# A five-block transformer in 32-bit: split projections against projections on the operands as they land

## The chip, the cores and the metric

The kernel runs on one core of one Trainium2 chip, as one launch. The metric is the time of that launch on the device in microseconds, the median over repeated runs; lower is better. Inputs, weights and output are 32-bit floating point.

## The reference

`x` has 256 tokens of 1024 features. It passes four layers, each a mixer and a gated feed-forward part (2816 wide), and then a fifth block with its own context of 256 tokens. In each layer six vectors of 1024 come from a matrix-vector product, and they shift, scale and gate:

```
mod = silu(c) @ ada_w[i] + ada_b[i]                  # 1024 x 6144, 24 MB
sh1, sc1, g1, sh2, sc2, g2 = split(mod, 6)
h = rms_norm(x, gain) * (1 + sc1) + sh1
x = x + g1 * mixer_i(h)                              # stick-breaking, MoBA, sliding window, stick-breaking
h = rms_norm(x, gain) * (1 + sc2) + sh2
x = x + g2 * ((silu(h @ w_gate) * (h @ w_up)) @ w_down)
```

The fifth block modulates `x` and the context, projects both with `w_in_2`, runs window attention and a bidirectional gated delta rule, joins them through `w_br_attn_2`, `w_br_dn_2`, `w_out_2`, and ends in `relu(h @ w_mlp1_2)^2 @ w_mlp2_2`. All weights are 32-bit and each is read once; the page counts 390 MB of reads.

## The kernel before

**Units.** Every projection is cut into units. A unit is one transfer of four blocks of 128 x 512 weights (1 MB) into a slot of the ring `raw`, and the matrix products of these four blocks with both tiles of 128 tokens: eight products (activation block 128 x 128 as the loaded weights of TensorE, the weights' 128 x 512 streamed). A few units are narrower (256 or 32 columns) or have two blocks. `units` and `loads` (lines 595 to 661) are lists that are written at build time: which units, and in which order SP fetches them, mixed with the "ada" loads, 1 MB each, of the modulation matrices.

**The split.** In the feed-forward parts, the two stick-breaking mixers and the fifth block, a unit is multiplied in three products of a reduced 32-bit type (`F32R`). ACT writes a rounded copy `w_hi` of the slot (`convert`, line 925, the copy is L939), DVE the remainder `w_lo` (`convert`, its subtraction is L1443), and only then is the slot of `raw` given back (`raw_free`). There are two buffers of each. The activations are split alike: ACT writes `full`, then `h_hi` or `act_hi` (`split`, L965), DVE `h_lo` or `act_lo` (L1516), on semaphores `split_full`, `split_hi`, `split_lo`. PE then does, per block (`unit`, line 2149):

```
nc.tensor.matmul(banks[t][:, 0:n], x_hi[:, kt, ts], w_hi[:, u % 2, i, 0:n], start=st, stop=False)
nc.tensor.matmul(banks[t][:, 0:n], x_hi[:, kt, ts], w_lo[:, u % 2, i, 0:n], start=False, stop=False)
ins = nc.tensor.matmul(banks[t][:, 0:n], x_lo[:, kt, ts], w_hi[:, u % 2, i, 0:n], start=False, stop=en)
```

These are L2161, L2162 and L2163; `half_unit` in the stick-breaking mixer does the same on two blocks (L2414 to L2416). A unit of eight blocks-times-tiles is thus 24 products.

**The native form.** In the MoBA and the sliding-window mixer the units are multiplied as 32-bit operands straight from `raw` (`unit_as_landed`, L2367, and L2462 for the output projection). One such product leaves two records in the trace: the program has 64 of L2462, the trace 128.

**Modulation.** DVE accumulates `acc += ada_row_block * c` over the eight blocks of a third of a modulation matrix (L1496, 1 MB per operation; `acc_c` for the context), `modulation_units`, line 1483. PE then sums over the partitions with a product against ones (`modulation` of PE, L2209 for the gates, L2219 for the columns), ACT copies the result. Which accumulations stand between which units is in the tables `ADA_MIX` and `ADA_FF`: `ADA_MIX[l]` by unit of the mixer, `ADA_FF[l]` by unit of the feed-forward part.

**Order.** Each engine's program is written out by hand and runs in that order. SP: `loads` in order, each waiting until its slot of the ring (`RING = 4`) is free: for a native unit when PE is done, else when DVE has read it. DVE: conversions, accumulations, the elementwise steps of attention (`SB_SLOTS`, `MOBA_DVE`, `SWA_DVE`), residuals and norms, interleaved by unit. Between layers stands a norm: residual (L1588, L1594), squares on ACT, scale on DVE (`n_st`, L1553), 32 transposes on PE (L2177, L2184), modulation on ACT (L1004). Ahead of the fifth block SP waits until the fourth layer's last residual is written before it fetches the context and masks.

Of the kernel before, what the change touches and what calls it, by code (L numbers as in the profile page):

```python
# [10 lines left out]
F32 = mybir.dt.float32  # L11
F32R = mybir.dt.float32r
# [5 lines left out]
P = 128  # L18
# [10 lines left out]
RING = 4  # L29
# [21 lines left out]
class Walk:  # L51


    def __init__(self):
# [4 lines left out]
        self.low = 0  # L59
        self.native = 0  # L60
# [46 lines left out]
def build(nc, w, out):  # L107
    with ExitStack() as ctx:
# [18 lines left out]
        w_hi_t, w_hi_off = at("w_hi", 2 * 2048, F32R)  # L127
        w_hi = w_hi_t[:, :].rearrange("p (s k n) -> p s k n", s=2, k=UNIT_K)
        w_lo_t, w_lo_off = at("w_lo", 2 * 2048, F32R)
        w_lo = w_lo_t[:, :].rearrange("p (s k n) -> p s k n", s=2, k=UNIT_K)  # L130
        x_res = tile("x_res", NT * D).rearrange("p (t d) -> p t d", t=NT)
        h_hi_t, h_off = at("h_hi", KT * SEQ, F32R)
        h_hi = h_hi_t[:, :].rearrange("p (k n) -> p k n", k=KT)
        h32 = tile("h32", KT * SEQ, offset=h_off).rearrange("p (k n) -> p k n", k=KT)
        h_lo = tile("h_lo", KT * SEQ, F32R).rearrange("p (k n) -> p k n", k=KT)
        act_hi_t, act_hi_off = at("act_hi", FFT * SEQ, F32R)
        act_hi = act_hi_t[:, :].rearrange("p (k n) -> p k n", k=FFT)
        act32 = tile("act32", KT * SEQ, offset=act_hi_off).rearrange("p (k n) -> p k n", k=KT)
        act_lo_t, act_lo_off = at("act_lo", FFT * SEQ, F32R)
        act_lo = act_lo_t[:, :].rearrange("p (k n) -> p k n", k=FFT)  # L140
        gates = tile("gates", 2 * D).rearrange("p (g n) -> p g n", g=2)
        full_t, full_off = at("full", 2 * 512)
        full = full_t[:, :].rearrange("p (b n) -> p b n", b=2)
# [42 lines left out]
        v_st = tile("v_st", 2 * NT * 512, offset=act_lo_off + 8 * 1024).rearrange("p (b t n) -> p b t n", b=2, t=NT)  # L186
        rope_st = tile("rope_st", NT * 512, offset=act_hi_off + 8 * 1024).rearrange("p (t n) -> p t n", t=NT)
        aT_odd = tile("aT_odd", 3 * 512, offset=act_hi_off + 12 * 1024).rearrange("p (b n) -> p b n", b=3)
        rot_st = tile("rot_st", NT * 512, offset=act_hi_off + 18 * 1024).rearrange("p (t n) -> p t n", t=NT)
# [32 lines left out]
        AH, AL, AB, AC = act_hi_off, act_lo_off, acc_off, qk_off  # L222
# [26 lines left out]
        q_decT, u_st = by_round("q_decT", h_off), by_round("u_st", h_off + 8 * KB)  # L249
# [14 lines left out]
        hi_ready = sem("hi_ready")  # L264
        lo_ready = sem("lo_ready")
# [35 lines left out]
        split_full = sem("split_full")  # L301
        split_hi = sem("split_hi")
        split_lo = sem("split_lo")
# [112 lines left out]
        ADA_U = 3 * KT  # L416

# [91 lines left out]
        LAT_F = DEPTH * (2 * (KT // 2) + 4 + FF // 256) + KT  # L509
# [60 lines left out]
        ADA_MIX = [{}, {n: [(1, 2 * KT + i)] for i, n in enumerate((0, 1, 3, 5, 7, 9, 11, 13))}, {}, {}]  # L570
        FF_FREE = [n for n in range(2, 32) if n not in (20, 21, 22, 23)]
        ADA_FF = [{}, {}, {}, {}]
        for i in range(2 * KT):
            ADA_MIX[0].setdefault((0, 0, 1, 2, 3, 4, 5, 5, 6, 7, 8, 9, 10, 11, 12, 13)[i], []).append((0, KT + i))
        for l in range(DEPTH):
            twice = KT if l + 1 == LAT else 0
            count = ADA_U - sum(len(x) for x in ADA_MIX[l + 1].values()) if l + 1 < LAT else ADA_U
            for i in range(count):
                slot = 2 + (i + min(i, twice)) * 29 // (ADA_U + twice) if count == ADA_U else FF_FREE[i * len(FF_FREE) // count]
                ADA_FF[l].setdefault(slot, []).append((l + 1, i))  # L580

# [20 lines left out]
        def add(m, pieces, kts, what="unit"):  # L602
            units.append((what, [(c0, mm, c1, n) for c0, mm, c1, n in pieces], list(kts), sum(p[3] for p in pieces)))

        mixer_units = []
        for l in range(DEPTH):
            kind, w_in, w_out = mixer(l)
            form = "unit" if kind == "sb" else "native"
            for what, g, pieces in qkv_panels(kind):
                for h in range(2):  # L610
                    add(w_in, [(c0, w_in, c1, n) for c0, c1, n in pieces], range(4 * h, 4 * h + 4), form)
            for h in range(2):
                for n in range(2):
                    add(w_out, [(0, w_out, 512 * n, 512)], range(4 * h, 4 * h + 4), form)
# [25 lines left out]
        def more_units(n, n_mix):  # L640

            return 0 if n == 0 else 2 if n == n_mix - 1 else 1

# [4 lines left out]
        loads += [next(ahead), next(ahead)]  # L648
        for l in range(DEPTH):
            small.setdefault(len(loads), []).append(("mixer", l))  # L650
            n_mix = 2 * len(qkv_panels(KINDS[l])) + 4
            for n in range(n_mix):
                loads += [next(ahead) for _ in range(more_units(n, n_mix))]
                loads += [("ada", *a) for a in ADA_MIX[l].get(n, [])]
            for p in range(FF // 256):
                for pos in range(2 * p - 1 if p else 0, 2 * p + 1):
                    loads.append(next(ahead))
                    loads += [("ada", *a) for a in ADA_FF[l].get(pos, [])]
# [16 lines left out]
        def freed_by_dve(upto):  # L675

            return sum(load[0] != "native" for load in loads[:upto])
# [2298 lines left out]
```

## Time and profile before

| | us |
|---|---|
| median of 3 runs (2114.25 to 2118.66) | 2116.64 |
| profiled execution, span from first to last instruction | 2113.7 |
| median less span: what lies around it | 2.9 |
| PE busy | 1926.3 |
| DVE busy | 1342.8 |
| ACT busy | 917.3 |

The page gives no time of its own for the profiled execution beside the span; the 2.9 us are the median's excess over the span. A busy PE is not PE at its peak: records of consecutive products overlap, since a record holds a product's latency as well. What a product costs in a stream is read from the distance between the starts of two neighbours.

### The profile page before, as it was taken

The numbers are of one execution on the slowest core, as the hardware profiler recorded it, in microseconds if no ns is written. First come the engines' busy times: TensorE is split into PE (matmuls) and PEld (weight loads), VectorE is DVE, ScalarE is ACT, GpSimd is POOL, SyncE is SP. The second block draws the span as 40 slices with busy tenths as digits, with TensorE's granted clock in tenths as the row PEclk, the third lists the DMA queues.
The fourth block names the chain that finished last, engine by engine and source line by source line (L and its number), as shares of the span: only waits on it lengthen the run. The fifth ranks groups of instructions, "written<-read, shape, count | busy, mean of one in ns | idle before, by whom it ended". The sixth has DMA issues, their size and how long they took to land.

```text
span 2113.7 us, 33128 instructions
## 1 busy us (share of the span) xinstructions
PE 1926.3 (91%) x13890; PEld 1500.4 (71%) x13890; DVE 1342.8 (64%) x1412; ACT 917.3 (43%) x1367; POOL 112.5 (5%) x139
## 2 busy tenths in 40 slices
PE   4888999999899998899999898998999888798999
PEld 3666887655687764687777677777777777776877
DVE  6776775563587734588755578875537645366465
ACT  3555444332544334544355554435435321335443
POOL 1001000110100000100000100001000302000000
PEclk9998999999999999999999999998989999999999
DMA  8763886564599931599933367983123000234552
GB/s 321 287 224 116 277 284 238 202 209 144 186 338 313 334 104 60 169 338 316 343 112 122 116 201 257 320 307 131 58 86 120 2 4 4 83 111 150 172 185 102
DMA packets 215401, 393.37 MB, mean 186 GB/s; under 512 B 11337, under 2 KB 130133, under 8 KB 199893
## 3 DMA queue, kind: packets, MB, share of 16 engines
q1 hardware_dynamic: 214741, 391.12, 54.0%
q8 instruction: 111, 1.82, 0.4%
q14 instruction: 37, 0.30, 0.0%
q0 software_dynamic: 512, 0.13, 0.0%
HBM read 390.17 MB, written 1.05 MB: 185 GB/s over the span
## 4 chain that ended last, share of the span: by engine, by line
PE 57%; DVE 24%; ACT 10%; issue 6%; DMA 2%; POOL 0%; DVEq 0%; ACTq 0%; SPq 0%; POOLq 0%
PE G L2161 12%; PE G L2163 11%; PE G L2162 11%; DVE w_lo L1443 11%; PE G L2367 6%; DVE acc L1496 5%; ACT w_hi L939 5%; PE G L2462 2%; PE A L2756 2%; ACT full L1004 1%; PE G L2770 1%; DMA raw<-in_ffn_w_down 1%; DVE act_st L1781 1%; PE A L2768 1%; DVE n_st L1553 1%
## 5 line engine op out<-in xcount | busy, mean ns | idle before, releaser
L1443 DVE TENSOR_TENSOR w_lo<-raw,w_hi 128x2048 fp32r<-128x2048 f32 (+2 forms) x237 | 513.4, 2166 | 285.4 <-ACT w_hi L939 274.8
L939 ACT CAST w_hi<-raw 128x2048 fp32r<-128x2048 f32 (+1 forms) x230 | 427.7, 1860 | 532.7 <-PE G L2163 479.8
L2161 PE MATMUL G<-w_hi,h_hi 128*128 128x512 f32 (+2 forms) x1232 | 491.3, 399 | 29.6 <-DVE w_lo L1443 12.1
L2163 PE MATMUL G<-w_hi,h_lo 128*128 128x512 f32 (+2 forms) x1232 | 480.9, 390 | 0.0
L2162 PE MATMUL G<-w_lo,h_hi 128*128 128x512 f32 (+2 forms) x1232 | 480.6, 390 | 0.0
L1496 DVE SCALAR_TENSOR_TENSOR acc<-raw,c_col,acc 128x2048 f32<-128x2048 f32 x120 | 282.0, 2350 | 43.3 <-DMA raw<-in_ada_w 22.5
L2161 PEld LDWEIGHTS G<-w_hi,h_hi 128*128 128x128 f32 x1232 | 235.0, 191 | 85.1 <-issue 40.0
L2163 PEld LDWEIGHTS G<-w_hi,h_lo 128*128 128x128 f32 x1232 | 234.1, 190 | 49.3
L2162 PEld LDWEIGHTS G<-w_lo,h_hi 128*128 128x128 f32 x1232 | 235.4, 191 | 45.1
L2161 PE MATMUL G<-w_hi,act_hi 128*128 128x512 f32 (+2 forms) x624 | 243.8, 391 | 24.0 <-DVE w_lo L1443 21.6
L2163 PE MATMUL G<-w_hi,act_lo 128*128 128x512 f32 (+2 forms) x624 | 241.0, 386 | 0.0
L2162 PE MATMUL G<-w_lo,act_hi 128*128 128x512 f32 (+2 forms) x624 | 240.8, 386 | 0.0
L2161 PEld LDWEIGHTS G<-w_hi,act_hi 128*128 128x128 f32 x624 | 118.8, 190 | 54.0 <-issue 28.4
L2163 PEld LDWEIGHTS G<-w_hi,act_lo 128*128 128x128 f32 x624 | 118.8, 190 | 23.7
L2162 PEld LDWEIGHTS G<-w_lo,act_hi 128*128 128x128 f32 x624 | 119.0, 191 | 22.6 <-issue 0.2
L2367 PE MATMUL G<-raw,h 128*128 128x512 f32 (+1 forms) x288 | 119.7, 572 | 0.0
L2367 PEld LDWEIGHTS G<-raw,h 128*128 128x128 f32 x288 | 54.4, 192 | 57.3 <-issue 56.5
L1516 DVE TENSOR_TENSOR act_lo<-full,act_hi 128x512 fp32r<-128x512 f32 (+1 forms) x78 | 52.1, 678 | 52.0 <-ACT act_hi L965 43.5
L2219 PE MATMUL A<-consts,acc 128*128 128x1 f32 x320 | 40.9, 262 | 23.6 <-DVE acc L1496 23.6
L2219 PEld LDWEIGHTS A<-consts,acc 128*128 128x128 f32 x320 | 41.7, 211 | 25.6 <-DVE acc L1496 23.8
L2462 PE MATMUL G<-raw,act 128*128 128x512 f32 x128 | 56.7, 593 | 0.0
L1004 ACT ACTIVATE full<-A,mod,gsc 128x128 f32<-128x128 f32 (+1 forms) x108 | 45.3, 489 | 21.6 <-DVE gsc L1532 13.7
(402 smaller groups left out, 2097.4 us busy)
## 6 DMA issues: line engine op xcount, KB each, us to landing
raw<-in_ada_w SPq DMA_DIRECT2D x96, 1024.0 KB, 5.1
raw<-in_ffn_w_gate SPq DMA_DIRECT2D x88, 512.0 KB, 4.0
raw<-in_ffn_w_up SPq DMA_DIRECT2D x88, 512.0 KB, 5.1
raw<-in_ffn_w_down SPq DMA_DIRECT2D x40, 1024.0 KB, 5.2
raw<-in_w_mlp SPq DMA_DIRECT2D x32, 1024.0 KB, 5.3
raw<-in_w_ada SPq DMA_DIRECT2D x24, 1024.0 KB, 5.4
raw<-in_w_in SPq DMA_DIRECT2D x18, 1024.0 KB, 5.3
raw<-in_sb_w_in SPq DMA_DIRECT2D x32, 512.0 KB, 4.8
```

What stands on the lines that cost most here:

```text
L939: nc.scalar.copy(w_hi[:, c % 2, 0:len(kts), 0:n], raw[:, slot].rearrange("p (k n) -> p k n", k=UNIT_K)[:, 0:len(kts), 0:n])\
L1004: return nc.scalar.activation(dst, src, ACT.Identity, scale=gsc[:, l % 2, gain + c:gain + c + 1], bias=mod[:, l % 2, which + c:which + c + 1])
L1443: return nc.vector.tensor_tensor(w_lo[:, c % 2, ks, 0:n], raw[:, slot].rearrange("p (k n) -> p k n", k=UNIT_K)[:, ks, 0:n], w_hi[:, c % 2, ...
L1496: nc.vector.scalar_tensor_tensor(out=acc_of(l, j), in0=raw[:, slot], scalar=c_col[:, c:c + 1], in1=acc_of(l, j), op0=ALU.mult, op1=ALU.add ...
L1516: nc.vector.tensor_tensor(dst_lo, full[:, f % 2, 0:n * dst_lo.shape[1]].rearrange("p (a n) -> p a n", n=n), dst_hi.bitcast(F32), ALU.subtr ...
L2161: nc.tensor.matmul(banks[t][:, 0:n], x_hi[:, kt, ts], w_hi[:, u % 2, i, 0:n], start=st, stop=False)
L2162: nc.tensor.matmul(banks[t][:, 0:n], x_hi[:, kt, ts], w_lo[:, u % 2, i, 0:n], start=False, stop=False)
L2163: ins = nc.tensor.matmul(banks[t][:, 0:n], x_lo[:, kt, ts], w_hi[:, u % 2, i, 0:n], start=False, stop=en)
L2219: ins = nc.tensor.matmul(banks[0][:, i:i + 1], x[:, c * P:c * P + P], ones[:, 0:1], start=True, stop=True)
L2367: ins = nc.tensor.matmul(banks[t][:, 0:n], h32[:, kt, t * P:t * P + P], raw[:, slot].rearrange("p (k n) -> p k n", k=UNIT_K)[:, i, 0:n], s ...
L2462: ins = nc.tensor.matmul(G[2 * (po[n] % 2) + t], act32[:, 2 * j + i, t * P:t * P + P], raw[:, slot].rearrange("p (k n) -> p k n", k=UNIT_K ...
L2756: ins = nc.tensor.matmul(A[c][half_of(1 - ch), cols_of(h)], LT[half_of(ch), c, cols_of(h)], X[half_of(ch), c, cols_of(h)], start=True, sto ...
```

## The change

- `convert` and `split` are gone on ACT and DVE, with `w_hi`, `w_lo`, `h_lo`, `act_lo` and their semaphores. ACT writes `hT` or `actT` in one operation (`put`), semaphore `panel_in`.
- PE's `unit` waits for the landed slot and does one product per block and tile, on 32-bit operands, for every projection: all are in the native form.
- The ring has seven slots. A unit's slot is free when PE is done with it, an ada load's when DVE is.
- The ada loads stand elsewhere: 16 of the 24 of a layer are accumulated in its own mixer (8 in the sliding-window layer), the first 8 (or 16) in the feed-forward part before; before, 16 stood in the first mixer, 8 in the second and none in the others. The last 8 of the fifth block are accumulated beside its first four units (`ADA_LAT`).
- Some tiles of the fifth block (`X`, `wu`, `u_st`) get a place of their own, `solve`.

```diff
-RING = 4
+RING = 7
...
+        ADA_MIX, ADA_FF, ADA_LAT = [{}, {}, {}, {}], [{}, {}, {}, {}], {}
+        for l, slots, own in ((0, 14, 2 * KT), (1, 14, 2 * KT), (2, 8, KT), (3, 14, 2 * KT)):
+            for i in range(own):
+                ADA_MIX[l].setdefault(i * slots // own, []).append((l, ADA_U - own + i))
+        for l, slots, ahead in ((0, 30, KT), (1, 30, 2 * KT), (2, 30, KT), (3, 22, 2 * KT)):
+            for i in range(ahead):
+                ADA_FF[l].setdefault(2 + i * slots // ahead, []).append((l + 1, i))
+        for i in range(KT):
+            ADA_LAT.setdefault(i // 2, []).append((LAT, 2 * KT + i))
...
-            def split(dst_hi, emit_full):
-                f, b = k.f, k.low
+            def put(ins):
                 k.f += 1
-                k.low += 1
-                if b >= 2:
-                    act.wait_ge(split_lo, b - 1)
-                n = dst_hi.shape[-1]
-                emit_full(full[:, b % 2, 0:n * dst_hi.shape[1]]).then_inc(split_full, 1)
-                act.wait_ge(split_full, f + 1)
-                nc.scalar.copy(dst_hi, full[:, b % 2, 0:n * dst_hi.shape[1]].rearrange("p (a n) -> p a n", n=n)).then_inc(split_hi, 1)
+                ins.then_inc(panel_in, 1)
...
-            def unit(x_hi, x_lo, kts, banks, first, last, n=512, done=gemm_done, ready=None, tiles=False):
-
-                u = nth_converted[k.u]
-                k.u += 1
-                pe.wait_ge(hi_ready, u + 1)
-                pe.wait_ge(lo_ready, u + 1)
+            def weights(slot):
+
+                return raw[:, slot].rearrange("p (k n) -> p k n", k=UNIT_K)
+
+            def unit(x, kts, banks, first, last, n=512, done=gemm_done, ready=None, tiles=False, again=False):
+
+                if not again:
+                    k.u += 1
+                    k.load = k.next_load(loads, "unit")
+                slot, count, _ = k.load
+                pe.wait_ge(landed[slot], count)
                 for t in range(NT):
-                    ts = slice(t * P, t * P + P)
                     if ready is not None:
-                        pe.wait_ge(split_lo, ready[t] - k.native)
+                        pe.wait_ge(panel_in, ready[t])
                     for i, kt in enumerate(kts):
-                        st = first and i == 0
-                        en = last and i == len(kts) - 1
-                        nc.tensor.matmul(banks[t][:, 0:n], x_hi[:, kt, ts], w_hi[:, u % 2, i, 0:n], start=st, stop=False)
-                        nc.tensor.matmul(banks[t][:, 0:n], x_hi[:, kt, ts], w_lo[:, u % 2, i, 0:n], start=False, stop=False)
-                        ins = nc.tensor.matmul(banks[t][:, 0:n], x_lo[:, kt, ts], w_hi[:, u % 2, i, 0:n], start=False, stop=en)
+                        ins = nc.tensor.matmul(banks[t][:, 0:n], x[:, kt, t * P:t * P + P], weights(slot)[:, i, 0:n],
+                                               start=first and i == 0, stop=last and i == len(kts) - 1)
```

Three places show how the engines' programs move. The first is DVE in the first layer's feed-forward part: `act_st` is the product of gate and up, `acc` the modulation sums. Before:

```order
L1443 TENSOR_TENSOR w_lo<-raw,w_hi 128x2048 x2
L1781 TENSOR_TENSOR act_st<-G,silu_st 128x256 x2
L1443 TENSOR_TENSOR w_lo<-raw,w_hi 128x2048
L1516 TENSOR_TENSOR act_lo<-full,act_hi 128x512
L1496 SCALAR_TENSOR_TENSOR acc_101<-raw,c_col,acc_101 128x2048
L1443 TENSOR_TENSOR w_lo<-raw,w_hi 128x2048
L1781 TENSOR_TENSOR act_st<-G,silu_st 128x256 x2
```
and now, the same stretch:

```order
L1346 SCALAR_TENSOR_TENSOR acc_97<-raw,c_col,acc_97 128x2048
L1603 TENSOR_TENSOR act_st<-G,silu_st 128x256 x4
L1346 SCALAR_TENSOR_TENSOR acc_97<-raw,c_col,acc_97 128x2048
L1603 TENSOR_TENSOR act_st<-G,silu_st 128x256 x4
L1346 SCALAR_TENSOR_TENSOR acc_97<-raw,c_col,acc_97 128x2048
```
All conversions and splits have left it, and fewer accumulations stand between the `act_st`. An `act_st` row now stands for two panels where nothing comes between them.

The second is SP at the start of the fifth block (`in_w_in` are its units, `in_w_ada` its modulation loads, `in_ctx` the context, which waits for the last residual of layer four). Before:

```order
L765 DMA raw<-in_w_in 128x4x512 x2
L765 DMA raw<-in_w_in 128x4x256
L736 DMA ctx_raw<-in_ctx 128x2x1024
L737 DMA mask_st<-in_masks 128x1216
L738 DMA rope_cs<-in_rope 128x4x64
L739 DMA rope_g<-in_q_norm_g 128x64
L740 DMA rope_g<-in_k_norm_g 128x64
L741 DMA sinks<-in_attn_sink 128x8
L742 DMA dn_rows<-in_a_log 128x16
L743 DMA dn_rows<-in_dt_bias 128x16
L744 DMA dn_rows<-in_dn_norm_g 128x64
L765 DMA raw<-in_w_in 128x4x256
```
and now:

```order
L734 DMA raw<-in_w_in 128x4x512
L705 DMA ctx_raw<-in_ctx 128x2x1024
L706 DMA mask_st<-in_masks 128x1216
L707 DMA rope_cs<-in_rope 128x4x64
L708 DMA rope_g<-in_q_norm_g 128x64
L709 DMA rope_g<-in_k_norm_g 128x64
L710 DMA sinks<-in_attn_sink 128x8
L711 DMA dn_rows<-in_a_log 128x16
L712 DMA dn_rows<-in_dt_bias 128x16
L713 DMA dn_rows<-in_dn_norm_g 128x64
L738 DMA raw<-in_w_ada 128x2048 x2
L734 DMA raw<-in_w_in 128x4x512
```
Only one unit is fetched ahead of the context now, not three, and two ada loads stand between the first unit and the second.

The third is DVE behind the context's norm, in the same place (`aq` is the query panel, `ss` its squared sums). Before:

```order
L1553 TENSOR_SCALAR n_st<-ctx_raw,rms_t 128x1024
L1443 TENSOR_TENSOR w_lo<-raw,w_hi 128x4x256
L1532 SCALAR_TENSOR_TENSOR gsc<-mod,cols 128x8
L1516 TENSOR_TENSOR act_lo<-full,act_hi 128x4x128 x2
L1443 TENSOR_TENSOR w_lo<-raw,w_hi 128x4x256
L1516 TENSOR_TENSOR act_lo<-full,act_hi 128x512 x2
L1828 TENSOR_REDUCE ss_84<-lrot 128x16
L1523 TENSOR_SCALAR rms_v<-ss_84 128x16
```
and now (the rows after these, up to the rotated `aq`, are as before, and two more `acc` rows stand behind them):

```order
L1395 TENSOR_SCALAR n_st<-ctx_raw,rms_t 128x1024
L1374 SCALAR_TENSOR_TENSOR gsc<-mod,cols 128x8
L1346 SCALAR_TENSOR_TENSOR acc<-raw,c_col,acc 128x2048 x6
L1634 TENSOR_REDUCE ss_80<-lrot 128x16
L1365 TENSOR_SCALAR rms_v<-ss_80 128x16
```
Six accumulations now stand ahead of the query's norm and two behind it; all eight are due before PE can sum the block's gates.

## Rows read from the trace of the kernel before

**Rows 1.** The page: span; busy time by engine; GB/s in 40 slices.
```profile
span 2113.7 us, 33128 instructions
...
PE 1926.3 (91%) x13890; PEld 1500.4 (71%) x13890; DVE 1342.8 (64%) x1412; ACT 917.3 (43%) x1367; POOL 112.5 (5%) x139
...
GB/s 321 287 224 116 277 284 238 202 209 144 186 338 313 334 104 60 169 338 316 343 112 122 116 201 257 320 307 131 58 86 120 2 4 4 83 111 150 172 185 102
```
**Rows 2.** Timeline, PE: start, length (us), engine, line, operation, tiles, shapes.
```profile
1463.01 0.28 PE L2161 MATMUL G<-w_hi,h_hi 128*128 128x256 f32 x1
...
1468.65 0.28 PE L2163 MATMUL G<-w_hi,act_lo 128*128 128x256 f32 x1
...
1870.05 0.39 PE L2161 MATMUL G<-w_hi,act_hi 128*128 128x512 f32 x1
...
1884.79 0.39 PE L2163 MATMUL G<-w_hi,act_lo 128*128 128x512 f32 x1
```
**Rows 3.** Chain that ended last, in order of time: start, length (us), work.
```profile
399.76 27.47 PE G L2367 x64
...
428.10 6.87 PE G L2367 x16
```
**Rows 4.** Groups by shape, PE: count, busy us, mean ns, idle before, releasers.
```profile
L2161 PE MATMUL G<-w_hi,h_hi 128*128 128x512 f32 x1200 | 482.5, 402 | 29.6 <-DVE w_lo L1443 12.1 <-issue 8.8 <-DVE h_lo L1516 8.5
...
L2161 PE MATMUL G<-w_hi,act_hi 128*128 128x512 f32 x592 | 234.2, 396 | 22.9 <-DVE w_lo L1443 21.6 <-ACT dz L1235 1.1
...
L2414 PE MATMUL G<-w_hi,act_hi 128*128 128x512 f32 x16 | 6.6, 415 | 1.5 <-DVE act_lo L1516 1.1 <-DVE w_lo L1443 0.4
```
**Rows 5.** Waits of PE: who waited for whom, us in total, times, longest.
```profile
PE G L2161 <- DVE w_lo L1443: 33.7, 22, 3.3
PE A L2177 <- DVE n_st L1553: 27.4, 13, 4.2
PE A L2219 <- DVE acc L1496: 23.6, 1, 23.6
PE G L2161 <- issue: 8.8, 6, 2.0
PE G L2161 <- DVE h_lo L1516: 8.5, 14, 1.3
...
PE A L2497 <- DVE act_st L1781: 6.2, 6, 3.0
...
PE A L2904 <- DVE hid_st L2105: 3.5, 8, 0.5
```
**Rows 6.** Timeline in the first mixer, DVE and PE.
```profile
52.42 2.29 DVE L1443 TENSOR_TENSOR w_lo<-raw,w_hi 128x2048 fp32r<-128x2048 f32 x1 [0.22 <-DVE acc L1496]
...
54.81 0.47 PE L2161 MATMUL G<-w_hi,h_hi 128*128 128x512 f32 x1 [1.23 <-issue]
```
**Rows 7.** Timeline of the norm behind the second mixer, DVE.
```profile
543.74 1.21 DVE L1443 TENSOR_TENSOR w_lo<-raw,w_hi 128x1024 fp32r<-128x1024 f32 x1
...
545.10 0.16 DVE L1543 SCALAR_TENSOR_TENSOR rms_v<-ssq,ssum 128x1 f32<-128x1 f32 x1 [0.15 <-DVE w_lo L1443]
```
**Rows 8.** The page's costliest groups, DVE: count, busy us, mean ns.
```profile
L1443 DVE TENSOR_TENSOR w_lo<-raw,w_hi 128x2048 fp32r<-128x2048 f32 (+2 forms) x237 | 513.4, 2166 | 285.4 <-ACT w_hi L939 274.8
...
L1496 DVE SCALAR_TENSOR_TENSOR acc<-raw,c_col,acc 128x2048 f32<-128x2048 f32 x120 | 282.0, 2350 | 43.3 <-DMA raw<-in_ada_w 22.5
```
**Rows 9.** Stretches: length, busy (instructions) of PE, PEld, DVE, ACT, POOL, clock, DMA, GB/s.
```profile
397.00:545.00 148.00, 145.44 (x536) 75.34 (x536) 74.71 (x123) 49.01 (x131) 19.58 (x21) 0.98 0.51 171
545.00:748.00 203.00, 193.62 (x875) 157.35 (x875) 155.77 (x113) 92.89 (x109) 5.80 (x9) 0.99 0.83 290
```
**Rows 10.** Timeline of the start of the last block, DVE and PE.
```profile
1468.77 1.88 PE L2209 MATMUL A<-acc,consts 128*128 128x512 f32 x4
...
1473.62 1.29 DVE L1856 TENSOR_TENSOR aq<-lrope_st,lrot 128x512 f32<-128x512 f32 x2 [2.88 <-POOL lrot L879]
...
1477.38 0.77 PE L2161 MATMUL G<-w_hi,h_hi 128*128 128x512 f32 x1 [3.26 <-DVE w_lo L1443]
```

More of the change, by code:

```diff
@@ L984, in squares, with norm @@
                 ins.then_inc(ss_ready, 1)
-            def norm(l, which, gain, dst=h_hi, x=x_res, x_end=None, piece=None, ahead=lambda: None, between=lambda: None, native=False):
+            def norm(l, which, gain, dst=hT, x=x_res, x_end=None, piece=None, between=lambda: None):
                 m = k.m
@@ L1211, in _ @@
                 k.panel("dve")
[L1214 removed]
+            norm(LAT, 0, 0, x_end=4 * LAT, piece="c0")
             def square(x, n, dst):
@@ L1533, in gains, with norm @@
                                                       in1=cols[:, col:col + 8], op0=ALU.add, op1=ALU.mult)
-            def norm(x=x_res, lo=h_lo, hi=h_hi, gain=lambda: None, ahead=lambda: None, between=lambda: None, last=None, native=False):
+            def norm(x=x_res, gain=lambda: None, last=None):
                 m = k.m
@@ L1561, in norm @@
                 scale_rows(0)
-                if last is not None:
-                    convert_half(1)
                 mean_square(1)
                 scale_rows(1)
-                ahead()
                 gain()
-                if native:
-                    between()
-                    return
-                for t in range(NT):
-                    split(lo[:, 0:KT // 2, t * P:t * P + P], hi[:, 0:KT // 2, t * P:t * P + P])
-                between()
-                for q in range(KT // 4, KT // 2):
-                    split(lo[:, 2 * q:2 * q + 2], hi[:, 2 * q:2 * q + 2])
             def last_residual(t, u_end, gate, l):
@@ L1742, in gains2 @@
                     gains(l, 8, 24, c_gain + 8).then_inc(gsc_ready, 1)
-                if l == 0:
-                    norm(gain=gains1, ahead=convert, between=convert)
-                else:
-                    norm(gain=gains1, between=convert, last=last, native=kind != "sb")
+                norm(gain=gains1, last=last)
                 panels = qkv_panels(kind)
-                u0 = k.u - 2
+                u0 = k.u
                 nq = 2 * len(panels)
+                k.u += nq + 4 + FF_UNITS
                 for n in range(nq + 4):
@@ L1818, in gains_ctx @@
                 gains(LAT, 16, 40, 88).then_inc(gsc_ready, 1)
-            norm(gain=gains_lat, between=convert, last=last)
-            norm(ctx_raw, act_lo, act_hi, gain=gains_ctx, ahead=convert, between=convert)
-            u0 = k.u - 4
+            norm(gain=gains_lat, last=last)
+            norm(ctx_raw, gain=gains_ctx)
+            u0 = k.u
             def head_norm(step):
@@ L2108, in hidden @@
                 dve.sem_inc(free_dve, 1)
-            def split_hidden(p):
-                for q in range(2):
-                    kt = 4 * (p % 4) + 2 * q
-                    split(act_lo[:, kt:kt + 2], act_hi[:, kt:kt + 2])
             for part in range(2):
@@ L2355, in step_softmax @@
                     pe.wait_ge(qT_ready, k.turned)
-                    pe.wait_ge(split_full, k.f)
+                    pe.wait_ge(panel_in, k.f)
                     weighted_values(n, g, evac, kind)
-            def unit_as_landed(kts, banks, first, last, n, ready):
-                k.u += 1
-                slot, count, _ = k.next_load(loads, "native")
-                pe.wait_ge(landed[slot], count)
-                for t in range(NT):
-                    pe.wait_ge(split_full, ready[t])
-                    for i, kt in enumerate(kts):
-                        ins = nc.tensor.matmul(banks[t][:, 0:n], h32[:, kt, t * P:t * P + P], raw[:, slot].rearrange("p (k n) -> p k n", k=UNIT_K)[:, i, 0:n],
-                                               start=first and i == 0, stop=last and i == len(kts) - 1)
-                ins.then_inc(gemm_done, 1)
             def sb_mixer(l, kind):
@@ L2452, in softmax_mixer @@
                     if j % 2 == 0:
-                        slots = [k.next_load(loads, "native") for _ in range(2)]
-                    pe.wait_ge(split_full, f_o[j])
+                        slots = [k.next_load(loads, "unit") for _ in range(2)]
+                    pe.wait_ge(panel_in, f_o[j])
                     for n in range(2):
```

433 lines of the change are left out of this document (115 added, 318 removed).

## The prediction

> **What bounds the kernel now.** I read the page's busy times first [rows 1]: PE 1926 of 2114 us, DVE 1343, ACT 917. PE is the candidate, but its share is no proof, because records overlap. So I read the timeline next [rows 2]: from 1870.05 to 1884.79 us lie 66 starts of 512-column products without a hole, 14.74 us over 65 steps, 0.2268 us each. A split triple costs 0.680 us. The groups by shape [rows 4] say how many there are: 1200 + 592 + 16 = 1808 triples of 512 columns, so 1808 x 0.680 = 1230 us of PE's time. The waits [rows 5] say what PE lacks beside that: its idle time is 2113.7 - 1926.3 = 187 us in all, and the list names the conversions as only a part of it. The kernel is bound by PE's stream of products. The conversions are long (513 us of DVE in `w_lo` [rows 8]) but nearly all of it runs beside PE; what they cost is what PE waits for.
>
> **The price of the native form.** The two mixers in the middle already use it. In the chain, 64 records take 27.47 us and 16 take 6.87 us [rows 3]; 0.429 us a record, and two records are one product, so one product is 0.858 us. It replaces three of 0.227. At the same granted clock (0.98 and 0.99 [rows 9]) the native form is dearer by 0.858 - 0.680 = 0.178 us per block and tile, a full unit 6.87 us instead of 5.44. The whole prediction hangs on this difference.
>
> The Trainium skill speaks against the change in the same direction: FP8 and Floating Point Precision, section TensorE Precision Notes, says that true FP32 takes four passes through the array. With this trace's split product as the pass it would be 4 x 0.2268 = 0.907 us and not 0.858. The measurement of the native form decides, and the sum goes by 0.858.
>
> **Added, on PE, all on the path:**
> - 1808 triples of 512 columns: 1808 x 0.178 = +322 us.
> - 32 triples of 256 columns. They run 48 starts in 5.64 us [rows 2], 0.120 each, 0.360 a triple. A native one is half of a 512-column one, 0.429: 32 x 0.069 = +2 us.
> - 32 triples of 32 columns, which no native row shows. The nearest are the 256-column ones: at most the same difference, +2 us; at the other end three of 0.120 become two, 32 x 0.120 = -4 us. I take 0, between the two.
>
> Sum +324 us.
>
> **Removed.**
> - Waits of PE for a converted weight [rows 5]: 33.7 us in 22 waits for `w_lo`, and 8.8 in 6 that the list calls issue. Of these the first mixer shows one: `w_lo` ends at 52.42 + 2.29 = 54.71 and PE starts at 54.81 [rows 6], so I count them as the same wait. Idle is counted from the end of a record, which lies 0.16 us behind the next start of a full stream, so 28 x 0.16 = 4.5 is added: -47 us. The rest of the 513 us of DVE and the casts of ACT lie beside PE and give nothing.
> - Waits for split activations: 8.5 us for `h_lo` in 14, 1.1 for `act_lo` at L2414 [rows 4, 5], and 14 x 0.16: -12 us. ACT now writes the operand itself.
> - `act_st` (6.2 us in 6) and `hid_st` (3.5 in 8) [rows 5] come late because DVE has a `w_lo` in front. The first goes, with its 1 us of overlap; of the second I take 1: -8 us.
> - The norms. DVE does half a conversion between the scale of one tile and the second mean square: `w_lo` starts at 543.74, and `rms_v` follows at 545.10 [rows 7]. Nine norms have that, each with PE waiting for `n_st`: 9 x 1.4 = -13 us of the 27.4 [rows 5]. The remainder, residual to squares to root to scale, stays. So does the 23.6 us wait for the first modulation.
>
> Sum -80 us. Bounds: -45 (the waits for weights alone) to -164 (all idle but the first 23.6 us).
>
> **Moved.** SP fetches in the new order, seven ahead. A feed-forward part had 34 unit slots and up to 24 ada loads: 290 GB/s over 203 us [rows 9] is 59 MB. It now has 34 + 16 at most, in about 203 + 264 x 0.178 = 250 us, near 205 GB/s; DMA gets slack, and I take no wait for it. The accumulations at 2.35 us [rows 8] move into the mixers. In the MoBA mixer eight more make 19 us on a DVE that is busy 74.7 of 148 [rows 9]; the sliding-window one gets eight where it had none. PE's next attention step queues behind them in DVE's order, and I take +5 us for both, between 0 and all sixteen exposed, 38 us. At the fifth block's start the last eight accumulations stand after the context's norm, six ahead of the query's norm, two behind it (the third place shown). PE began the sums of the gates at 1468.77, and DVE ended the query's norm at 1473.62 + 1.29 = 1474.9 [rows 10]. Two accumulations then take until 1479.6; PE's own units there grow by 5 us (two of 1.43 and 32 x 0.069), and DVE's query by the first 3 of these. So PE's sums start at about 1483 where they could at 1474: +9 us, bounds 0 and 8 x 2.35 = 19. The `w_lo` wait of 3.26 behind it [rows 10] is in the 47. The order that SP runs in there lets only one unit ahead of the context; the next one comes behind two ada loads, some 4.6 MB after the residual, 14 us at the 338 to 343 GB/s of the busiest slices [rows 1], and PE has the norm's transposes, a unit of 6.87 us and the context's sums to do until it needs it: 0.
>
> Sum +14 us.
>
> **Total.** 324 - 80 + 14 = +258. The profiled span becomes 2113.7 + 258 = 2372, and with the 2.9 us by which the median exceeds the span, 2374 us, slower by 12%.
>
> **Rivals.**
> 1. *The fast stream (faster).* In the mixers a native record could be held up by something beside the array (weight loads, attention steps next to it), and in the long dense loops two records could cost 0.227 each. Then a product is 0.454, and the time is 2374 - 1808 x 0.404 = 1643 us. It decides from 0.858 - 258 / 1808 = 0.715 us per product down. Against it: 64 records back to back in 27.47 us are already a dense stream [rows 3], and all runs of 16 have the same 6.87.
> 2. *A dearer product in the dense loops.* If a native product took four times the 0.2268 us of a split one there, 0.907 instead of 0.858, it would be 1808 x 0.049 = +89, 2463 us. The same rows speak against it. It is what the page named above would give.
> 3. *Much more cover comes off.* ACT and DVE lose over half of their work, and every chain between PE's steps could shorten: with all idle but the first wait gone, 84 us more than I take, 2290 us. For it: attention steps also queue behind conversions. Against it: the pure chains (norms, the delta rule) hold most of the rest.
> 4. *Accumulations on the path.* The 24 that moved into the second and third mixers and the fifth block, at 2.35 + 0.22 us each, stand fully in PE's way: 62 us in place of 14, 2422 us. For it: DVE's order is strict. Against it: DVE is half idle there [rows 9].
>
> That the change doesn't do what it says is excluded by the programs: no `w_lo`, `h_lo` or `act_lo` row is left in them.
>
> **Chances.** The forecast 0.80; rival 1 0.01, rival 2 0.04, rival 3 0.07, rival 4 0.07; no change at all 0.01. The range takes in the forecast's own unknowns (more of the idle gone, about 35 us; accumulations exposed, about 35 us) and the near parts of rivals 3 and 4: 2340 to 2410. Some 0.2% (4 us) is what a measurement of this kernel can tell from no change: faster 0.01, the same 0.01, slower 0.98.
>
> **What would show it.** Starts of L1937 0.429 us apart in the feed-forward parts, two records per product, and a unit of 6.87 us: else the main term is wrong. A feed-forward part of about 203 + 47 - 8 = 242 us. DVE busy below 830 us (1343 - 513). PE's waits for `n_st` near 14 us, none for weights but a few for `raw`. At the fifth block a wait of some 9 us in front of the gates' sums. PE busy in the mixers with a DVE `acc` as releaser would be rival 4; waits for `raw<-in_ffn` by PE would say that SP's order or the ring binds, which I have at nothing.

## The result

The changed kernel takes **2326.61 us** (median of 4 runs, 2324.59 to 2329.43), beside 2117.65 us for the kernel before on the same chip: a ratio of 1.0981, 95% interval 1.0959 to 1.1004. It is slower by 209 us. I forecast 2374 us and 2340 to 2410; the direction and the main term hold, and the time lies 13 us below the range. Among all runs in this document one of `a_ring4` (8170 us) and one of the kernel before (3045 us) were far slower than the others of the same kernel, and the medians leave these two out.

The page of the changed kernel, the lines that answer to [rows 1], and its chain and costliest groups (busy us, mean ns of one, idle before and its releaser):

```profile
span 2325.0 us, 27802 instructions
...
PE 2214.2 (95%) x12018; PEld 1161.3 (50%) x12018; DVE 756.0 (33%) x1061; ACT 439.7 (19%) x1023; POOL 116.2 (5%) x139
...
PE 91%; DVE 4%; issue 2%; ACT 1%; DMA 1%; POOL 0%; SPq 0%; DVEq 0%; ACTq 0%; POOLq 0%
...
L1937 PE MATMUL G<-raw,hT 128*128 128x512 f32 (+2 forms) x2752 | 1189.0, 589 | 3.4 <-DMA raw<-in_w_in 3.4
...
L1937 PE MATMUL G<-raw,actT 128*128 128x512 f32 (+2 forms) x1248 | 523.6, 579 | 0.0
```

DVE went from 1343 to 756 us and ACT from 917 to 440, and PE's idle time from 187 to 111 us. So the program does what the change says, and PE is busy 288 us longer.

The price of a block is as forecast. This is the chain in order of time (start, length, work) in the first feed-forward part, and PE's timeline in the same part:

```profile
196.67 20.75 PE G L1937 x47
217.42 0.44 PE A L2257 x4
217.86 13.74 PE G L1937 x32
231.59 0.44 PE A L2257 x4
```

```profile
299.72 2.74 PE L1937 MATMUL G<-raw,hT 128*128 128x512 f32 x6
302.29 0.60 PE L2257 MATMUL A<-consts,act_st 128*128 128x128 f32 x4
302.73 0.59 PE L1937 MATMUL G<-raw,hT 128*128 128x512 f32 x1
```

32 records in 13.74 us are 0.429 each, and six from 299.72 until the transpose starts at 302.29 are 0.428: the rate of the middle mixers [rows 3], now in the dense loops. The transpose follows at once.

The stretches of the second mixer and of the feed-forward part behind it, after (length; busy time and instructions of PE, PEld, DVE, ACT, POOL; granted clock; share of DMA; GB/s), the same as [rows 9]:

```profile
438.40:587.50 149.10, 145.20 (x535) 74.83 (x534) 90.07 (x133) 47.47 (x133) 24.92 (x22) 0.98 0.65 226
587.50:827.90 240.40, 239.97 (x625) 111.91 (x624) 56.09 (x57) 24.89 (x61) 2.35 (x7) 0.99 0.63 210
```

The feed-forward part is 240.4 us (242 forecast) with PE busy all of it. What PE waits for in the changed kernel (us, times, longest), beside [rows 5]:

```profile
PE A L1994 <- DVE acc L1346: 23.3, 1, 23.3
PE G L2529 <- issue: 12.3, 8, 1.9
PE A L2527 <- issue: 11.4, 8, 1.6
PE A L1952 <- DVE n_st L1395: 11.3, 11, 2.7
PE A L1984 <- DVE acc L1346: 6.4, 1, 6.4
...
PE G L1937 <- DMA raw<-in_w_in: 3.4, 1, 3.4
```

The waits for `w_lo`, `h_lo`, `act_st` and `hid_st` are gone, `n_st` fell from 27.4 to 11.3, and the wait before the fifth block's gates' sums (L1984) is there with 6.4 us.

### The profile page after: what moved, and what is told of

The parts are those of the page before. It is cut to its first block, busy times and chain, and to the rows that moved or that the text cites. A ratio compares the mean times of both kernels' runs of the same rounds, so it can differ in the third digit from the quotient of the medians.

```text
span 2325.0 us, 27802 instructions
## 1 busy us (share of the span) xinstructions
PE 2214.2 (95%) x12018; PEld 1161.3 (50%) x12018; DVE 756.0 (33%) x1061; ACT 439.7 (19%) x1023; POOL 116.2 (5%) x139
## 4 chain that ended last, share of the span: by engine, by line
PE 91%; DVE 4%; issue 2%; ACT 1%; DMA 1%; POOL 0%; SPq 0%; DVEq 0%; ACTq 0%; POOLq 0%
PE G L1937 71%; PE G L2223 2%; PE A L2515 2%; DVE acc L1346 1%; PE A L2527 1%; PE G L2529 1%; PE A L2257 1%; PE A L2055 1%; PE A L1984 1%; DVE n_st L1395 1%; PE A L1959 1%; PE A L2105 1%; DMA raw<-in_w_in 1%; PE A L2038 1%; PE G L2176 1%
## 5 line engine op out<-in xcount | busy, mean ns | idle before, releaser
L1937 PE MATMUL G<-raw,hT 128*128 128x512 f32 (+2 forms) x2752 | 1189.0, 589 | 3.4 <-DMA raw<-in_w_in 3.4
L1937 PEld LDWEIGHTS G<-raw,hT 128*128 128x128 f32 x2752 | 519.6, 193 | 602.9 <-issue 597.1
L1937 PE MATMUL G<-raw,actT 128*128 128x512 f32 (+2 forms) x1248 | 523.6, 579 | 0.0
L1937 PEld LDWEIGHTS G<-raw,actT 128*128 128x128 f32 x1248 | 233.8, 190 | 278.5 <-issue 277.0
L2223 PE MATMUL G<-raw,actT 128*128 128x512 f32 x128 | 56.7, 593 | 0.0
L2529 PE MATMUL G<-XT,Z 64*64 64x64 f32 x1280 | 43.2, 220 | 12.3 <-issue 12.3
L944 ACT ACTIVATE hT<-A,mod,gsc 128x128 f32<-128x128 f32 (+1 forms) x120 | 47.3, 516 | 13.6 <-DVE gsc L1374 11.9
L2529 PEld LDWEIGHTS G<-XT,Z 64*64 64x64 f32 x1280 | 39.7, 134 | 13.3 <-issue 13.3
L2515 PE MATMUL A<-X,LT 64*64 64x64 f32 x1280 | 41.3, 219 | 1.8 <-issue 1.5
L2515 PEld LDWEIGHTS A<-X,LT 64*64 64x64 f32 x1280 | 39.4, 135 | 2.8 <-issue 2.7
```

Source lines behind the costliest of these rows:

```text
L944: return nc.scalar.activation(dst, src, ACT.Identity, scale=gsc[:, l % 2, gain + c:gain + c + 1], bias=mod[:, l % 2, which + c:which + c + 1])
L1937: ins = nc.tensor.matmul(banks[t][:, 0:n], x[:, kt, t * P:t * P + P], weights(slot)[:, i, 0:n], start=first and i == 0, stop=last and i == ...
L2223: ins = nc.tensor.matmul(G[2 * (po[n] % 2) + t], actT[:, 2 * j + i, t * P:t * P + P], weights(slot)[:, 2 * (j % 2) + i], start=j == 0 and ...
L2515: ins = nc.tensor.matmul(A[c][half_of(1 - ch), cols_of(h)], LT[half_of(ch), c, cols_of(h)], X[half_of(ch), c, cols_of(h)], start=True, sto ...
L2529: ins = nc.tensor.matmul(G[c][half_of(ch if last else 1 - ch), hs], Z[half_of(1 - ch), c, hs], XT[half_of(1 - ch), c, hs], start=True, sto ...
```

## The experiments

The question was where 47 us of my sum lie. Three theories: the conversions cost PE more than I had taken from the list of waits; the ring of seven slots or the new layout of the loads gave something; TensorE's granted clock did. All kernels ran beside the kernel before, whose median was 2116.3, 2118.7, 2117.8 and 2119.2 us in the four sets. Kernels that leave out conversions or halves of operands compute wrong values; only their times are used.

### Conversions taken out of the kernel before

`b_w`: no low part of the weights is computed.

```
-  nc.tensor.matmul(banks[t][:, 0:n], x_hi[:, kt, ts], w_lo[:, u % 2, i, 0:n], start=False, stop=False)
+  nc.tensor.matmul(banks[t][:, 0:n], x_hi[:, kt, ts], w_hi[:, u % 2, i, 0:n], start=False, stop=False)
...
-  pe.wait_ge(lo_ready, u + 1)
...
-  low_part(c, slot, slice(0, len(kts)), n).then_inc(lo_ready, 1)
```

> The kernel before, without VectorE's subtraction for the weights' low part: the second product of each triple reads the high part instead, so that TensorE does the same three products of the same size but waits only for ScalarE's cast. ScalarE and the activations are as before. My recorded sum gives this the 47 us of waits for weights (less those that go on to wait for the cast), 13 us in the norms and 8 us of act_st and hid_st: about -68, 2050 us. The rival that conversions cost more than the list of waits names (short waits inside the projections, and clock lost around them) expects -85 to -105, 2013 to 2033 us.

Measured: 2021.8 us, ratio 0.9544 (0.9518 to 0.9569): -95 us, as the rival said; my sum gave -68.

`b_a`: activations are written once, by ACT, as the rounded operand.

```
-  emit_full(full[:, b % 2, 0:n * dst_hi.shape[1]]).then_inc(split_full, 1)
-  nc.scalar.copy(dst_hi, full[...]).then_inc(split_hi, 1)
+  emit_full(dst_hi).then_inc(split_full, 1)
...
-  nc.vector.tensor_tensor(dst_lo, full[...], dst_hi.bitcast(F32), ALU.subtract).then_inc(split_lo, 1)
```

> The kernel before, with the activations written once: ScalarE writes the high part itself, there is no second copy and no subtraction on VectorE, and the third product reads the high part again. Weights are converted as before. My recorded sum: -12 us, 2105 us. Rival (hidden costs): -20 to -35, since ScalarE's second copy also stands in its order ahead of casts and attention steps: 2083 to 2097 us.

Measured: 2094.8 us, ratio 0.9892 (0.9864 to 0.992): -22 us, where I had -12.

`b_wa`: both.

> Both edits together: three products per block and only ScalarE's cast of the weights is left of the conversions. My recorded sum: -80, 2037 us. The theory that the recorded step Removed was too small by itself: -105 to -125, about 2003 us, and the time in the cold clock falls to about 90 us as in the changed kernel. The rival that the surplus came from the seven-slot ring and the new order of loads: still about -80 here.

Measured: 2005.6 us, ratio 0.9466 (0.9437 to 0.9496): -111 us, where I had -80. It still has four slots, the old layout and ACT's casts of the weights, so neither ring nor layout is in this number.

Where do the 27 us more of `b_w` come from? PE's waits in `b_w`:

```profile
PE A L2211 <- DVE acc L1489: 23.3, 1, 23.3
PE A L2169 <- DVE n_st L1546: 16.7, 11, 3.8
...
PE G L2153 <- DVE h_lo L1509: 6.8, 12, 1.2
```

The listed waits for weights (33.7 and 8.8) and for `act_st` (6.2) and `hid_st` (3.5) are gone, and `n_st` fell by 10.7, which is 63 us together. The page of `b_w` gives PE's whole idle time:

```profile
span 2017.3 us, 32566 instructions
...
PE 1905.0 (94%) x13890; PEld 1503.2 (75%) x13890; DVE 834.4 (41%) x1175; ACT 917.5 (45%) x1367; POOL 108.8 (5%) x139
```

That is 112 us idle, where the kernel before has 187: 75 us less. So 12 us more than those 63 are idle time in rows that my sum had not touched (the delta rule's steps that the list calls issue, `h_lo`, attention steps). The other 21 us of the 96 by which the span is shorter are a fall of PE's busy time, from 1926.3 to 1905.0. The transposes of `act_st`, L2497 before, show how a late start can hide there. Timeline of the kernel before, then of `b_w`, a last product of a unit and the transpose behind it:

```profile
252.10 0.39 PE L2163 MATMUL G<-w_hi,h_lo 128*128 128x512 f32 x1
...
252.58 0.66 PE L2497 MATMUL A<-consts,act_st 128*128 128x128 f32 x4
```

```profile
252.01 0.39 PE L2155 MATMUL G<-w_hi,h_lo 128*128 128x512 f32 x1
252.24 0.60 PE L2488 MATMUL A<-consts,act_st 128*128 128x128 f32 x4
```

In `b_w` the transpose starts 0.23 us behind the product, in the kernel before 0.48. The product's record ends at 252.49, so only 0.09 us of the 0.25 lost lies open, and the row has no idle time put to it. Of the 44 such places all start within 0.230 to 0.232 us in `b_w`; before, 32 of the 44 take over 0.30. Summed over the starts they lose 11 us, where the list has 6.2 in 6. (Some 2 us of the 21 are the clock: 55 products of 512 columns have a record of 0.60 us or more in `b_w`, as at the lower level, and 64 before, at 0.2 us each dearer.) Summed in the same way, start to start over all of PE's records, `b_w` gains 57 us at projection products (waits for the weights; I had 47), 20 at what stands behind a unit (attention steps, `act_st`, `hid_st`; I had 8) and 20 among the other steps (11 of them at `n_st`, 6 at the delta rule's `X`; I had 13). So about 12 of the surplus are idle time that I didn't count, and some 15 are overlap beyond the 5.5 us that my terms had for it. Of the three terms, those for the weights and for `act_st` and `hid_st` were short; the one for `n_st` (13) was about right, and what came beside it lies in steps for which I had nothing.

The clock is not the cause of what the projections gained. `b_wa` has 94 us at the lower level (1.2 GHz) where before has 122, but its projections' products of 512 columns with a record of 0.60 us or more are 66, against 64. What the 28 us fewer at the lower level gave elsewhere, in transposes and short steps, was not measured apart.

### The same removal from the other side

`a_b3`: the changed kernel with three 16-bit products in place of one 32-bit product. They read the upper half of each operand, in place, and leave out the lower.

```
-  ins = nc.tensor.matmul(banks[t][:, 0:n], x[:, kt, t * P:t * P + P], weights(slot)[:, i, 0:n], ...)
...
+  for r in range(3):
+      ins = nc.tensor.matmul(banks[t][:, 0:n], upper(x[:, kt, t * P:t * P + P]), upper(weights(slot)[:, i, 0:n]), ...)
```

> The changed kernel, with every projection block that was split before done by three 16-bit products on the upper halves of the same landed operands, in place of one 32-bit product; nothing is converted, the sixteen-bit reads step over the lower halves. The projections of the two middle mixers stay 32-bit, as before. If the whole difference is the price of the blocks and a 16-bit product costs the 0.227 us of the rounded one: 2326.6 - 321 = 2005 us, equal to the kernel before without conversions (2005.6). If a product without the rounded type costs a quarter of 0.859, 0.215 us: 1808 x 0.036 = 65 less, 1940 us. If the seven-slot ring and the new order of loads had their own part in the result, it misses 2005 by that part.

Measured: 1994.4 us, ratio 0.9418 (0.9404 to 0.9433). Its products are cheaper than the rounded ones in two places. Those of 512 columns started every 0.225 us and not every 0.2268: 5424 x 0.0018 = 10 us. The 96 products of 32 columns started every 0.025 us and not every 0.112; from the first of them to the next step PE took 5.8 us, where `b_wa` took 15.3: another 10. At the same rates it would be 2014, which is 312 us below the 2326.6 of the changed kernel. The price of the blocks is 1808 x (2 x 0.4293 - 3 x 0.2267) = 323, with +2 for 256 columns and -4 for 32 columns, 321. The 9 us between the two are about what PE waits more in `a_b3`: 129.5 us idle, some 8 of them places where the trace lacks a record, against 110.8. So the price of the blocks is shown to within some 10 us here; against `b_wa` the changed kernel is 321.0 us dearer, and there the agreement is two things that cancel, as the next three kernels show.

### Layout of the loads and size of the ring

`a_old`: the changed kernel, tables of the modulation loads as before. `a_ring4`: the changed kernel with four slots. `a_old4`: both.

```
-  for l, slots, own in ((0, 14, 2 * KT), (1, 14, 2 * KT), (2, 8, KT), (3, 14, 2 * KT)):
+  ADA_MIX, ADA_LAT = [{}, {n: [(1, 2 * KT + i)] for i, n in enumerate((0, 1, 3, 5, 7, 9, 11, 13))}, {}, {}], {}
...
-RING = 7
+RING = 4
```

> The changed kernel with the modulation loads laid out as before: all of a block's in the feed-forward part ahead, eight in the MoBA mixer, none in the fifth block. My recorded step Moved: -14 us, 2312 us (5 in the two middle mixers, 9 in the fifth block). After the kernel before without conversions came out at -111, which with +321 leaves nothing for Moved: 0 within 4 us. If the feed-forward parts now choke on loads (24 in 34 slots, but 250 us long): slower by up to 10 us.

> The changed kernel with a landing ring of four slots instead of seven, order of loads unchanged. Forecast: TensorE frees a slot only at the end of a unit of 6.87 us, and a unit of 2 MB lands in about 6 us at 340 GB/s, so four slots are enough nearly everywhere: +0 to +5 us. If the seven slots carry the kernel through the stretches with an accumulation behind each unit: +10 to +40 us, as waits of TensorE for raw.

A unit is 1 MB and not the 2 MB written there.

> The changed kernel with both the old layout of modulation loads and a ring of four slots. With the new layout the ring of four cost 12 us (2338.3 against 2326.6) and the new layout with seven slots cost 18 (2326.6 against 2309.0). If the two are independent: 2309 + 12 = 2321 us. If seven slots are only needed where accumulations stand between the mixers' units: 2309 to 2313 us. The kernel before without conversions has four slots, the old layout and 2005.6 us; with the dearer blocks, 321, that is 2326.6 us less what ScalarE's casts still cost there.

The 2338.3 and the 12 us in this one are 2334.5 and 8 in the table, and 10 by the ratios.

| us (ratio to before) | seven slots | four slots |
|---|---|---|
| old layout | 2309.0 (1.088 to 1.0917) | 2325.3 (1.0956 to 1.0996) |
| new layout | 2326.6 (1.0959 to 1.1004) | 2334.5 (1.0997 to 1.1059) |

The new layout costs 18 us with seven slots: my step gave 14. It lies where I put it. From one norm's transposes to the next, `a_old` against the changed kernel: second mixer 146.5 against 149.1 us, third 106.9 against 111.6, and 7.6 longer from the fifth block's first norm to its last. With four slots the new layout costs less, 9 us by the medians and 11 by the ratios, so layout and ring don't simply add. With old layout and four slots 16 us are lost, and here the list shows them, in `a_old4`:

```profile
PE G L1939 <- DMA raw<-in_ffn_w_down: 15.5, 7, 4.3
```

`a_old` and the changed kernel have no such wait. The reason can be read in who frees a slot. What SP waited for in the kernel before, and in `a_old4` (us, times, longest):

```profile
SPq L765 <- DVEq L1461: 873.4, 163, 19.3
```

```profile
SPq L736 <- PE G L1939: 1330.3, 178, 30.7
```

Before, DVE's conversion frees the slot (L1461) while PE still has the unit ahead of it; the converted copies are two more units in stock. In the native form a slot is held until its last product, and with four slots PE waits for `raw`; the list of `b_wa` has no such wait.

`a_old4` is the kernel to lay beside `b_wa`: both have four slots and the old layout, and they differ by the price of the blocks, by ACT's casts and by that stock. `b_wa` at the price of the blocks is 2005.6 + 321 = 2326.6, and `a_old4` measures 2325.3. So the casts that are gone and the stock that is gone cancel to about 1 us; what each is worth by itself was not measured. The seven slots then give 16 us (`a_old4` to `a_old`), and the new layout takes 18 (`a_old` to the changed kernel): that is why the changed kernel lies so close to `b_wa` plus 321. In the two middle mixers, native in every kernel, `b_wa` takes 147.8 and 111.9 us, `a_old4` 147.1 and 109.6, `a_old` 146.5 and 106.9: of the 6 us there the ring gives 3.

### One product

`a_b1`: as `a_b3`, with one product.

> The changed kernel with one 16-bit product per block in the parts that were split before (its results are not usable), to see what lies under the products. Two products of 0.227 fewer in each of 1808 blocks: 2005 - 820 = 1185 us if all were still TensorE's stream. The loads are about 390 MB, 1150 us at 340 GB/s, and the attention chains lie bare: I expect 1300 to 1500 us, with TensorE waiting for raw as the largest idle.

Measured: 1536.4 us, ratio 0.7255: a little above the range expected. Stretches of the first and second feed-forward parts:

```profile
143.70:257.00 113.30, 85.63 (x349) 40.41 (x357) 35.08 (x48) 24.61 (x61) 2.91 (x8) 0.85 0.98 344
407.10:540.90 133.80, 91.47 (x350) 41.31 (x357) 54.27 (x56) 24.67 (x61) 7.31 (x11) 0.83 1.00 358
```

DMA is busy 98 and 100% at 344 and 358 GB/s: under PE's stream lies the transfer, at 113 to 134 us in such a part, far below the 240 of the changed kernel. In the changed kernel nothing but PE's products binds these parts.

### Versions that could beat both

`b_half`: the kernel before, both halves of the norms' conversion behind the gains. `b_half1`: only the second half, as in this edit.

```
   scale_rows(0)
-  if last is not None:
-      convert_half(1)
   mean_square(1)
   scale_rows(1)
   ahead()
   gain()
+  if last is not None:
+      convert_half(1)
```

> The kernel before, with only one move: in the nine norms the two halves of the weight conversion, 1.2 to 1.3 us each, stand behind both row scales and the gains instead of ahead of the two mean squares. If they stood in the chain as my step for the norms says, and TensorE reaches the first unit later than the moved conversion: -13 us, 2104 us. If the conversion is then what the first unit waits for: 0 within 4 us, or slower by up to 10 us.

> The kernel before, with only the second half of the norms' weight conversion moved behind both row scales and the gains; the first half stays ahead of the first mean square. Moving both halves took 9 us off the starts around the norms' transposes and gave 8 back in the projections behind them, where more products ran at the low clock; it came out at 0.9977 of the kernel before, 2111.5 us. If it is the second half alone that stands in the chain (it lies between the first tile's scale and the second mean square) and the moved work is then only 1.2 us: -5 to -10 us, 2108 to 2113 us, better than both halves. If the clock falls later in the same way, the same 0.998 comes out; if the first half was what mattered, no difference from before.

Measured: `b_half` 2111.5 us, ratio 0.9977 (0.9963 to 0.9991); `b_half1` 2111.5, ratio 0.9970 (0.9956 to 0.9983). Both are faster than the kernel before, by 0.2 to 0.3%, and so than the changed one. In `b_half1`, the norm behind the second mixer, DVE:

```profile
539.11 1.64 DVE L1553 TENSOR_SCALAR n_st<-x_res,rms_t 128x1024 f32<-128x1024 f32 x1
540.66 0.14 DVE L1543 SCALAR_TENSOR_TENSOR rms_v<-ssq,ssum 128x1 f32<-128x1 f32 x1
...
543.33 1.21 DVE L1443 TENSOR_TENSOR w_lo<-raw,w_hi 128x1024 fp32r<-128x1024 f32 x1
```

The second mean square follows the scale at once, beside [rows 7]. From start to start, PE's transposes of `n_st` gain 10.4 us in `b_half1` and 9.2 in `b_half`. But 6.4 and 8.1 us go back in the projections. In `b_half` 111 of their products of 512 columns have a record of 0.60 us or more, as at the lower level, and 64 before, at 0.2 us each dearer: 9 us. In `b_half1` it is 76, 2 to 3 us, and what takes the other 4 is open. The granted clock (behind the five engines) is lower too in the fifth block's stretch from the first norm on, before and in `b_half1`:

```profile
1454.10:1590.00 135.90, 128.14 (x692) 103.87 (x691) 63.48 (x109) 54.91 (x110) 7.31 (x17) 0.92 0.23 74
```

```profile
1448.90:1585.00 136.10, 128.32 (x679) 104.63 (x678) 60.89 (x108) 54.79 (x110) 7.32 (x17) 0.90 0.21 68
```

`b_pool1`, `b_pool2`: the kernel before with one or two of four slices of the low part on GpSimd, in the feed-forward parts and the last MLP.

```
+  pool.wait_ge(hi_ready, c + 1)
+  pool.wait_ge(gemm_done, converted[c - 2] + 1)
+  nc.gpsimd.tensor_tensor(w_lo[:, c % 2, ks, 0:n], raw[:, slot]...[:, ks, 0:n], w_hi[:, c % 2, ks, 0:n].bitcast(F32), ALU.subtract).then_inc(pool_lo, 1)
```

> The kernel before, complete and with its own results, in which GpSimd subtracts one of the four slices of each weight conversion in the feed-forward parts and the last MLP (all but their first four units), and VectorE the other three. GpSimd's own 128x512 products of two tensors take 1.04 us and VectorE has 0.57 a slice, so VectorE is relieved by about 0.57 us in each of some 148 units, 84 us in all, and GpSimd is done before it. The parts concerned lost 9 to 11 us each to conversions in three, 26 in the fourth and 8 in the last: 64 us. If the loss goes with VectorE's load: -10 to -25 us, 2092 to 2107 us. If both engines slow each other at the same memory: VectorE's subtraction grows over 1.72 us and the time stays or rises.

> The same with two of four slices on GpSimd: 2.1 us there against 1.15 on VectorE, in units of 5.44 us. VectorE relieved by some 160 us. If its load is what counts: -20 to -40 us, 2077 to 2097 us. If GpSimd's 2.1 us behind the cast is then the later of the two, TensorE waits for it and the gain is smaller than with one slice.

Measured: 2128.6 us, ratio 1.004 (1.0012 to 1.0067), and 2172.5, ratio 1.0256 (1.0231 to 1.0281). Both slower. Timeline of `b_pool1`, DVE and POOL, at two places:

```profile
268.63 1.76 DVE L1472 TENSOR_TENSOR w_lo<-raw,w_hi 128x1536 fp32r<-128x1536 f32 x1 [2.70 <-ACT w_hi L968]
268.67 2.87 POOL L858 TENSOR_TENSOR w_lo<-raw,w_hi 128x512 fp32r<-128x512 f32 x1 [2.57 <-ACT w_hi L968]
...
280.02 1.29 POOL L858 TENSOR_TENSOR w_lo<-raw,w_hi 128x512 fp32r<-128x512 f32 x1 [2.54 <-ACT w_hi L968]
280.10 2.83 DVE L1472 TENSOR_TENSOR w_lo<-raw,w_hi 128x1536 fp32r<-128x1536 f32 x1 [0.22 <-ACT w_hi L968]
```

Where DVE is first, it takes 1.76 us and POOL 2.87; where POOL is first, it takes 1.29 and DVE 2.83. The second one's time is about the first one's plus its own, and the pair takes 2.91 us either way: one runs behind the other. Work moved to GpSimd still stands in VectorE's way here, at about twice the price a slice: the pair takes 1.15 us more than DVE's 1.76, and a slice costs DVE 0.57 to 0.59.

The Trainium skill (GPSIMD Engine Reference, section Specifications) says that GpSimd's way to SBUF is shared with VectorE, in contention with VectorE instructions that have two SBUF inputs. This subtraction has two, and the trace agrees, with 2.87 and 2.83 us in place of 1.29 and 1.76. An instruction with one SBUF input beside GpSimd was not tried.

## Why the prediction was wrong, point by point

- **The price of the native form: right.** 0.429 us a record in all dense loops. Added came to +321 (324 forecast); the narrow products of 32 columns were at the other end of my bounds. Rivals 1 and 2 fell with it. The Trainium skill (FP8 and Floating Point Precision, TensorE Precision Notes) says four passes. At 0.2268 each they would be 0.907; the two records measured here are 0.859. Whether four shorter passes lie in them no run here shows.
- **Removed: wrong, the failed step.** -80 forecast; `b_wa` measures -111 for the same conversions. I counted 72 us of idle time, from the rows that name a conversion or a tile behind one, and 8 us of overlap (0.16 us for some of the starts). PE's idle time in `b_wa` is 103.9 us (2003.0 - 1899.1), 84 less than before, and its busy time is 27 less. So of the 31 us missing some 12 are idle time in rows that I had left out, and some 19 are overlap of records: a start that is late by less than that is in no list. The norms' part, -13, was the size of what the transposes gain (10 to 11), but in `b_half` and `b_half1` part of it goes back in the projections. The bound of -164 held it; my range took only about 35 us of it.
- **Moved: right for the layout, wrong by omission for the ring.** The accumulations cost +18 (14 forecast), 7 in the middle mixers (5) and 8 in the fifth block (9), where the wait before the gates' sums is 6.4 us. That DMA would have slack was right for the changed kernel as it stands: PE waits 3.4 us for `raw` in all. But I priced the seven slots at nothing, without a reason. With four the same kernel is 10 us slower by the ratios, and 16 with the old layout. With casts and stock, which cancel, that is 18 us more off than `b_wa` shows (2326.6 to 2309.0 in `a_old`). This is the second term that was missing.
- **Rival 3 was the nearest.** Much more cover came off: of its 84 us beyond my sum about 49 came, 31 by the conversions and 18 by the ring. Its 2290 us lie 37 us from the measured time, my 2374 lie 47. I had said for it that attention steps also queue behind conversions; that was right in kind and small in size, 8 us in `b_w`, and the ring was not in its argument. It deserved more than 0.07. Its limit also held: the pure chains are still there (`n_st` 11.3, the delta rule 24 us in two rows).
- **Rival 4** had its mechanism and not its size: one exposed wait of 6.4 us and 7 us in the mixers, not 24 accumulations.

The sum with what was measured apart: 2005.6 (`b_wa`) + 321 (blocks) - 16 (ring) + 18 (layout) = 2329, measured 2326.6. The 2 us between are less than the spread of four runs. The forecast missed by 47: 49 us too little removed and 3 too much added, against 4 too little moved.

## What to carry to other kernels

When an engine's load is taken off a kernel whose other engine runs a dense stream, don't price it by those idle rows alone that name this load. In `b_w` they held 63 of 96 us. Rows that name something else, or issue, held another 12. The last 21, a fifth, lay in busy time: compare start-to-start times at each hand-over with the shortest seen at that place, since an overlap of records hides every lateness below it. A conversion between landing and use is also a buffer: when it goes, count the slots that it had freed early, and don't put a larger ring at nothing. And before moving work to GpSimd, look whether VectorE's instructions beside it read two SBUF operands.

## What the runs showed of the hardware

- From start to start, a 32-bit product of 512 columns is two records of 0.429 us, a rounded one a record of 0.227 and a 16-bit one of 0.225, with both operands read at a step of two elements: no dearer than the rounded one. At 32 columns the 32-bit record and the rounded one are both 0.112, and the 16-bit one (`a_b3`) is 0.025.
- VectorE and GpSimd serialize on a subtraction of two SBUF operands: 1.76 and 1.29 us as the first one, 2.83 and 2.87 as the second one.
- With PE waiting often (`a_b1`), the mean granted clock is 0.893, with PE dense 0.981: in `a_b1` 331 us lie at the lower level and in the changed kernel 92, so a kernel that is freed of its stream pays part of it back in the clock.
